# An expert stage that adds its rows in PSUM, reads the fullest expert's weights once, and loads down weights from ScalarE's queue

## The reference, cut to what matters

```python
# hier_moe: top-1 of 4 groups, then top-2 of its 8 experts; weight = p(group) * softmax of the two
hb = jax.nn.silu(xb @ w_gate[e]) * (xb @ w_up[e])        # 1024 -> 512, for each chosen (token, expert)
y  = (hb @ w_down[e]) * wr[:, None]                      # 512 -> 1024
h  = h + segment_sum(y, row_tok)                         # both experts of a token, on the residual
y_prompt, y_sample = rmsnorm(h, final_norm_g)
```

## Time and profile before

| | us |
|---|---|
| median of 3 runs | 1508.8 (1507.97 to 1509.42) |
| the profiled execution | 1504.2 |
| its span on the core | 1502.6 |
| PE busy | 1150.9 (77%) |
| DVE busy | 464.5 (31%) |
| ACT busy | 234.5 (16%) |
| POOL busy | 207.2 (14%) |
| bytes moved | 315.69 MB, 210 GB/s over the span |

### The profile page before, as it was taken

How to read it: one execution, slowest core, us unless ns; L and a number is a source line. 1 busy time by engine, 2 the same in 40 slices (tenths; PEclk the granted TensorE clock), 3 DMA queues, 4 the chain that set the end, 5 groups by cost and what they waited for, 6 DMA issues and landing times. The chain is left out here.

```text
span 1502.6 us, 22749 instructions
## 1 busy us (share of the span) xinstructions
PE 1150.9 (77%) x7953; PEld 729.8 (49%) x7953; DVE 464.5 (31%) x1117; ACT 234.5 (16%) x646; POOL 207.2 (14%) x402
## 2 busy tenths in 40 slices
PE   5899999999995898877899999666565656565650
PEld 3666667666763455554566664443232333232320
DVE  2235654656455574333000001331111111111113
ACT  1132233223322353222000000000000000000000
POOL 3033433344324111010000000000000000000003
PEclk9799999999997998999899999678887888787875
DMA  6033424332422226542965360299999999999963
GB/s 197 20 113 88 115 84 143 104 99 84 143 59 56 51 49 175 133 148 84 255 155 134 80 232 0 77 413 426 429 428 428 428 427 429 429 427 428 428 283 123
DMA packets 171882, 315.69 MB, mean 210 GB/s; under 512 B 22162, under 2 KB 153810, under 8 KB 159170
## 3 DMA queue, kind: packets, MB, share of 16 engines
q1 hardware_dynamic: 161842, 303.34, 56.1%
q0 software_dynamic: 2048, 6.95, 1.6%
q10 hardware_dynamic: 7952, 4.88, 1.1%
HBM read 296.02 MB, written 19.11 MB: 210 GB/s over the span
## 5 line engine op out<-in xcount | busy, mean ns | idle before, releaser
L1696 PE MATMUL ph<-w_gate_up,x_gathered 128*32 128x256 f32 x1408 | 121.8, 521 | 108.7 <-DMA w_gate_up<-in_w_exp_up 108.1
L669 PE MATMUL psg<-stretch 128*128 128x336 f32 x512 | 159.8, 477 | 11.3 <-DVE h_sample_out L647 9.6
L1696 PEld LDWEIGHTS ph<-w_gate_up,x_gathered 128*32 128x32 f32 x1408 | 60.5, 148 | 170.1 <-issue 98.1
L669 PEld LDWEIGHTS psg<-stretch 128*128 128x128 f32 x512 | 103.7, 204 | 69.2 <-DVE h_sample_out L647 15.4
L1664 DVE SCALAR_TENSOR_TENSOR h_gate<-h_tanh,ph 128x128 f32<-128x128 f32 x33 | 9.5, 287 | 387.3 <-ACT h_tanh L1624 387.3
L1696 PE MATMUL ph<-stretch,x_gathered 128*32 128x256 f32 x704 | 60.7, 519 | 57.9 <-DMA stretch<-in_w_exp_up 57.9
L584 DVE SCALAR_TENSOR_TENSOR x_conv<-x_padded,conv_wh,x_conv 128x360 f32<-128x360 f32 x96 | 56.9, 593 | 101.0 <-ACT x_conv L533 90.0
L678 PE MATMUL psg<-stretch 128*128 128x256 f32 (+1 forms) x384 | 84.5, 380 | 0.0
L1346 PE MATMUL psm<-stretch,w_merge 128*128 128x336 f32 x256 | 75.8, 455 | 6.9 <-DMA w_merge<-in_w_in 6.9
L1745 POOL DMA_INDIRECT y_expert<-expert_rows,slot_i x6 | 5.7, 958 | 505.8 <-PEq L1715 504.2
L678 PEld LDWEIGHTS psg<-stretch 128*128 128x128 f32 (+1 forms) x384 | 67.3, 177 | 14.5
(11 more groups left out here) (415 smaller groups left out, 1659.4 us busy)
## 6 DMA issues: line engine op xcount, KB each, us to landing
w_down<-in_w_exp_down SPq DMA_DIRECT2D x33, 2048.0 KB, 40.4
w_gate_up<-in_w_exp_gate SPq DMA_DIRECT2D x22, 2048.0 KB, 33.8
w_gate_up<-in_w_exp_up SPq DMA_DIRECT2D x22, 2048.0 KB, 38.4
stretch<-in_w_exp_gate SPq DMA_DIRECT2D x11, 2048.0 KB, 34.1
stretch<-in_w_exp_up SPq DMA_DIRECT2D x11, 2048.0 KB, 38.7
stretch<-in_w_in SPq DMA_DIRECT2D x16, 1024.0 KB, 5.3
stretch<-in_w_in SPq DMA_DIRECT2D x16, 512.0 KB, 7.5
h<-in_state_ssm SPq DMA_DIRECT2D x16, 512.0 KB, 4.8
```

The source lines that it names most:

```text
L669: mm = pe.matmul(ps[m][:, 0:T], wg[:, k, P * m:P * m + P], S["xnT"][:, k, :], start=(k == 0), stop=(k == KT - 1))
L1696: mm = pe.matmul(ph[h][32 * j:32 * j + 32, 0:256], xg[h][:, k, :], w_gu[w][:, :, k, P * j:P * j + P], start=(k == 0), stop=(k == KT - 1))
```

## The change

- The residual and the expert rows are summed in six PSUM banks (`acc`, "token_rows"). TensorE first puts the residual there with an identity (six matmuls at the start of routing), then, for each block, adds the block's rows with 12 matmuls: 32 rows of `back`, which holds the router weight where a token has this slot, times 32 rows of `y_block`. `expert_rows`, its blank write, its stores and its gather are gone, and so is `final_phase`: the norm reads the banks at the end of `moe_phase`, after six closing matmuls with zeros.
- Routing also spreads each token's two slots and two weights over all partitions as rows: products with the identity (VectorE and GpSimd), 12 matmuls with `ones`, four copies by ScalarE. VectorE makes `back` for each block from them.
- There are always 33 blocks. The fullest expert among 3 to 31 takes block 28 (the expert of that number goes to its place), and its pairs 33 to 64 are block 31, which computes with the weights that block 28 loaded; expert 31 is block 32. Overflow blocks beyond begin at 33. Every load takes its expert's number from `blk_e`.
- Down weights are issued by ScalarE, for block b + 3 after the copy of block b; gate and up stay with SyncE.
- `ph`'s two halves share one bank, `px` and `py` another.
- The loops: 4 x 6 blocks, blocks 24 to 32 written out, then 4 x 6 bodies under an If from block 33.

The diff, cut to its core:

```diff
+NMAIN = NE + 1
+TWICE, AGAIN = 28, 31
 NOVER = 20
-NBLK = NE + NOVER
+NBLK = NMAIN + NOVER
+ADD_ORDER = [(0, 0), (0, 1), (0, 2), (0, 3), (1, 0), (1, 1), (1, 2), (1, 3), (2, 0), (2, 2), (2, 1), (2, 3)]
...
-            sp.wait_ge(kx_ok, 1)
-            sp.dma_start(S["ydram"][NE * BLK:SLOTS, :].rearrange("(b p) d -> p b d", p=64),
-                         bc(blank[0:64].unsqueeze(1), [64, (SLOTS - NE * BLK) // 64, D])).then_inc(blank_out, 16)
...
-            v.memset(blank, 0.0)
...
 def route_phase(nc, A, S, sem):
...
+            for j in range(2):
+                pool.tensor_tensor(dgw[:, j, :, :], bc(S["ident"][:, :].unsqueeze(1), [P, 3, P]),
+                                   bc(S["topw"][:, :, j:j + 1], [P, 3, P]), ALU.mult).then_inc(dgw_ok, 1)
...
+            for j in range(2):
+                act.wait_ge(row_ps, j + 1)
+                act.activation(S["slot_row"][:, j, :], ps[j][:, 128:128 + T], ACT.Copy).then_inc(row_ev, 1)
+            for j in range(2):
+                act.wait_ge(row_ps, j + 3)
+                act.activation(S["weight_row"][:, j, :], ps[j][:, 128:128 + T], ACT.Copy).then_inc(row_ev, 1)
...
+            for j in range(4):
+                pe.matmul(acc[:, j, :], S["ident"][:, :], S["xtok"][:, 0:2, 256 * j:256 * j + 256],
+                          start=True, stop=False)
+            for i in range(2):
+                pe.matmul(acc[0:80, 4 + i, :], S["ident"][0:80, 0:80], S["xtok"][0:80, 2, 512 * i:512 * i + 512],
+                          start=True, stop=False)
             pe.wait_ge(mk, 1)
...
+            for src, ok, freed in ((dgs, dgs_ok, 0), (dgw, dgw_ok, 2)):
+                for j in range(2):
+                    pe.wait_ge(ok, j + 1)
+                    if freed:
+                        pe.wait_ge(row_ev, j + 1)
+                    for t, r in enumerate(ROWS):
+                        mm = pe.matmul(ps[j][:, 128 + COL[t]:128 + COL[t] + r], o[0:r, :], src[0:r, j, t, 0:r],
+                                       start=True, stop=True)
+                    mm.then_inc(row_ps, 1)
...
+            for j in range(2):
+                v.tensor_tensor(dgs[:, j, :, :], bc(S["ident"][:, :].unsqueeze(1), [P, 3, P]),
+                                bc(S["slot"][:, :, j:j + 1], [P, 3, P]), ALU.mult).then_inc(dgs_ok, 1)
...
 def moe_phase(nc, A, S, sem):
...
+        def loads(b):
+
+            return b // 3 + 1 - (1 if b >= AGAIN and b % 3 == AGAIN % 3 else 0)
+
         def each_block(eng, nblk, body):
-            sure = NE // UNROLL
+            sure = TWICE // UNROLL
             with eng.Fori(0, sure) as i:
                 for u in range(UNROLL):
-                    body(UNROLL * i + u, u, i)
-            with eng.Fori(sure, -(-NBLK // UNROLL)) as i:
+                    body(UNROLL * i + u, u, 2 * i + loads(u))
+            for b in range(sure * UNROLL, NMAIN):
+                body(b, b, loads(b))
+            with eng.Fori(0, -(-NOVER // UNROLL)) as i:
                 for u in range(UNROLL):
-                    with eng.If(UNROLL * i + u < nblk):
-                        body(UNROLL * i + u, u, i)
+                    with eng.If(UNROLL * i + u + NMAIN < nblk):
+                        body(UNROLL * i + u + NMAIN, u + NMAIN, 2 * i + loads(u + NMAIN), over=True)
...
                 act.wait_ge(y_ps, b + 1)
-                act.wait_ge(y_sent[h], 64 * (3 * i + u // 2) + 64)
-                act.activation(yr[h][:, :], py[h][:, 0:256], ACT.Copy).then_inc(y_ev, 1)
-                act.drain()
-                for j in range(4):
-                    act.dma_start(ydram[bass.ds(BLK * b, BLK), j, :], yr[h][32 * j:32 * j + 32, :]
-                                  ).then_inc(y_sent[h], 16)
+                act.wait_ge(added, b + 1)
+                act.activation(yr[h][:, :], py[:, :], ACT.Copy).then_inc(y_ev, 1)
+                def refill(column):
+                    e = act.value_load(S["blk_e"][0:1, column], min_val=0, max_val=NE - 1)
+                    load_down(act, A, S, u % 3, e)
...
+            def weights_back(b, h):
+                v.scalar_tensor_tensor(weq[:, :, :], slot_row[:, :, :], lane[:, 0:1], weight_row[:, :, :],
+                                       ALU.is_equal, ALU.mult)
+                v.drain()
+                v.wait_ge(added, b + 1)
+                v.tensor_tensor(back[h][:, :], weq[:, 0, :], weq[:, 1, :], ALU.add).then_inc(back_ok, 1)
+                v.tensor_scalar(lane[:, :], lane[:, :], float(BLK), None, ALU.add)
...
                 gather_rows(b + 2, 1 - h)
                 pe.wait_ge(ht_ok, b + 1)
-                pe.wait_ge(dn_in[w], 32 * i + 16 * (u // 3) + 16)
-                pe.wait_ge(y_ev, b)
+                pe.wait_ge(xt_ok, b + 2)
+                pe.wait_ge(dn_in[w], 16 * n)
+                pe.wait_ge(y_ev, b + 1)
...
                 mm.then_inc(y_ps, 1)
+                pe.wait_ge(y_ev, b + 2)
+                pe.wait_ge(back_ok, b + 1)
+                for t, j in ADD_ORDER:
+                    r, q = ROWS[t], slice(32 * j, 32 * j + 32)
+                    if (t, j) == (2, 1):
+                        mm.then_inc(tail_half, 1)
+                        pe.wait_ge(tail_half, b + 1)
+                    mm = pe.matmul(token_rows(t, j), back[h][q, COL[t]:COL[t] + r], yr[h][q, :], start=False,
+                                   stop=False)
+                mm.then_inc(added, 1)
...
+            for i in range(6):
+                r = P if i < 4 else 80
+                mm = pe.matmul(acc[0:r, i, 0:CLOSE], S["zeros"][:, 0:r], S["ident"][:, 0:CLOSE], start=False, stop=True)
+            mm.then_inc(all_added, 1)
```

More of the change, by code:

```diff
@@ L901, in _ @@
                     load_kv(2 * i + half, half, True)
-            sp.wait_ge(blank_out, 16)
         @block.gpsimd
@@ L1515, in _ @@
+            v.tensor_copy(rank[0:80, 2, :], ps[0][0:80, 64:96])
+            v.drain()
+            v.tensor_scalar(most[:, :], key[:, :], topn[:, 0:1], None, ALU.is_equal)
+            v.tensor_reduce(nb[:, :], over[:, :, :], AX.X, ALU.add)
+            v.drain()
+            v.tensor_tensor(far2[:, :], most[:, :], over[:, :, 0], ALU.mult)
+            v.tensor_tensor(key[:, :], most[:, :], to28[:, :], ALU.mult)
             v.tensor_scalar(late[:, :, :], rank[:, :, :], BLK - 0.5, None, ALU.is_gt)
@@ L1578, in moe_phase @@
+        pw = [ctx.enter_context(nc.psum_tensor(f"pw{h}", [P, 512], F32)) for h in range(2)]
+        ph = [pw[0][:, 256 * h:256 * h + 256] for h in range(2)]
+        px, py = pw[1][:, 0:256], pw[1][:, 256:512]
         sel_ok, xr_ps, xt_ok, gu_ps, th_ok, hb_ok, ht_ok, y_ps, y_ev = (
             sem(n) for n in ("sel_ok", "xrow_ps", "xt_ok", "gu_ps", "hth_ok", "h_ok", "ht_ok", "yb_ps", "yb_ev"))
-        y_sent = [sem("y_sent_even"), sem("y_sent_odd")]
-        ydram = S["ydram"].rearrange("s (j d) -> s j d", j=4)
+        back_ok, added, all_added, tail_half = (sem("weights_back_ok"), sem("rows_added"), sem("all_added"),
+                                                sem("tail_half_added"))
@@ L1619, in _, with body @@
             nblk = blocks_of(act)
-            def body(b, u, i):
+            act.dma_start(fg[:, :], A["final_norm_g"].partition_broadcast(P)).then_inc(g_in, 16)
+            def body(b, u, n, over=False):
                 h = u % 2
@@ L1625, in body @@
                 act.wait_ge(y_ps, b + 1)
-                act.wait_ge(y_sent[h], 64 * (3 * i + u // 2) + 64)
-                act.activation(yr[h][:, :], py[h][:, 0:256], ACT.Copy).then_inc(y_ev, 1)
-                act.drain()
-                for j in range(4):
-                    act.dma_start(ydram[bass.ds(BLK * b, BLK), j, :], yr[h][32 * j:32 * j + 32, :]
-                                  ).then_inc(y_sent[h], 16)
-            act.sem_inc(y_ev, 1)
-            act.sem_inc(y_sent[0], 64)
-            act.sem_inc(y_sent[1], 64)
-            each_block(act, nblk, body)
-            for h in range(2):
-                act.wait_ge(y_sent[h], 64 * ((nblk + (1 - h)) // 2) + 64)
-                act.sem_inc(S["pool_passed"])
+                act.wait_ge(added, b + 1)
[3 more added lines that the diff above has]
+                    load_down(act, A, S, u % 3, e)
+                if isinstance(b, int) and b + 3 < NMAIN:
+                    if b + 3 != AGAIN:
+                        refill(slice(b + 3, b + 4))
+                elif isinstance(b, int):
+                    with act.If(b + 3 < nblk):
+                        refill(slice(b + 3, b + 4))
+                elif u < TWICE // UNROLL * UNROLL and not over:
+                    refill(bass.ds(b + 3, 1))
+                else:
+                    with act.If(b + 3 < nblk):
+                        refill(bass.ds(b + 3, 1))
+            act.sem_inc(added, 2)
+            act.sem_inc(y_ev, 1)
+            each_block(act, nblk, body)
+            act.wait_ge(all_added, 1)
+            for t in (2, 0, 1):
+                r = ROWS[t]
+                act.activation(as_tile(xsq[0:r, :], t), tile_rows(t), ACT.Square,
```

(2 more changed lines are left out.)

264 lines of the change are left out of this document (155 added, 109 removed).

## The result

| | before | after |
|---|---|---|
| median, us | 1508.4 (1506.9 to 1509.4, 4 runs) | 1575.8 (1569.7 to 1578.7, 4 runs) |
| span of the profiled execution, us | 1502.6 | 1577.0 |
| PE busy, us | 1150.9 | 1216.0 |
| bytes moved, MB | 315.69 | 300.54 |

The changed kernel is slower: ratio 1.044, 95% interval [1.041, 1.048]. The forecast was 1492.7, faster. Lines are those of the changed kernel: gate/up L1868, gather L1858, down L1878, the adds L1888, the closing matmuls L1896.

The account below looks back on a forecast made before the run. The expert stage was taken as bound by weight transfers, the last blocks by TensorE. TensorE's end 1454.2 + 33.3 - 1.0 gave span 1486.5, 16.1 below 1502.6; from the median 1508.8, 1492.7 us, range 1484 to 1504.

Parts of the forecast that it names:

- The end: After TensorE's last block: skipped bodies 16.6 us, closing matmuls 2.4, the rest 14.3; 33.3 in place of 43.4, -10.1.
- the list of signs: What would show the forecast right or wrong: loads, queue rate, waits, block and add times, the gap before the closing matmuls.
- 1.0 for attention: Attention: VectorE's memset of the blank rows goes, from the path to TensorE's first matmul there: -1.0 us.
- Last blocks: Blocks 30 to 32: one load left but three blocks of 10.5 us; with 1.5 for landing order TensorE ends at 1454.2.
- The rival in which the tail hides: Last blocks: TensorE catches up and ends one block after the last byte, 8 us earlier, 1485; chance 0.12.
- The down-queue term: Expert stage: down loads on their own queue run ahead, so gate/up lands later by 0 to 4.9 us, 1.5 taken.
- Routing: Before the first refill: VectorE +4.0, residual +0.3, row products +6.2, warmer clock -1.5; refill at 1007.8, queue empty +8.7 us.
- Traffic: Expert stage's queue: one 6.29 MB load less, -14.7 us, and no 32 KB row stores, -10.1 us.
- The adds: Each block on TensorE: 12 adds, 24 passes, with four row groups overlapping, take 2.4 us; block 10.3, with slack 10.5.
- adds in a row: Rival for each block's adds: row groups don't overlap, block 13.9 us, last three cost 10.2 more, 1503; chance 0.12.
- TensorE as the bound: Rival for the expert stage: adds of 6.3 us make blocks 14.2; at 15 us a block, 1536, slower; chance 0.05.
- the load was dropped: Expert stage: the fullest expert's two blocks share one load; the rival that it isn't dropped gives 1500, chance 0.03.

Follow-up runs that it names:

- the one with nine adds: The changed kernel with nine adds of twelve in the bodies of its never-run second loop: 1577.7 us, one run.
- the versions with both edits: Changed kernel, one test ahead of the second loop, fullest expert at places 24 and 27, down loads on SyncE's queue: 1474.2 us; with TensorE's sure blocks written out, 1472.9.
- the version without the jumps: Changed kernel with one test, early pair, down loads on SyncE's queue, and TensorE's 24 sure blocks written out in place of a loop: 1472.9 us, ratio 0.977.
- its two versions: The kernel before with its second loop as two turns of twelve bodies, 1556.4 us; and with a test around each turn of that loop, 1502.5 us.

## Why the prediction was wrong

It failed in one step above all: *"The end. Skipping 21 bodies took up to 14.5 us, 0.69 each; now 24 are skipped: 16.6 (to 20 if it goes by TensorE's larger body)."* It measured 94.75 us. The row was read as a price per body and carried over by count. It held two things: 21 skips at about 0.32, and, as the rest, fetches of code. And that price holds only while the loop stays in what the sequencer keeps; the change made the body 12 matmuls longer, and no row of before showed where that ends. The bound from above, 20 us, took the length of the body for a factor; it should have asked what a loop of 72 matmuls a body costs if it is fetched in each turn. The trace of before had the means: 24 packets on the instruction queue, two of them in a window otherwise nearly empty. The Trainium skill (Advanced Engine Details and Errata, ISA Cache) gives TensorE a cache of 128 KB for its instructions, in lines of 16 KB; the prediction didn't draw on it. The trace agrees with the lines: the packets are of 16 KB. The size fits as far as the runs go: a loop of some 108 KB was kept, and one that takes 8 packets a turn, at most 128 KB, was not; the one with nine adds, some 123 KB by the estimate above, was not either, so the usable size lies below that or the estimate is off. No rival had it, though the list of signs named it ("more than 17 us between the last add and the closing matmuls").

The steps, from the forecast span of 1486.5 to the 1577.0 measured:

| step | forecast, us | measured, us | difference on the path |
|---|---|---|---|
| block 29's gate/up starts on TensorE | 1421.7 (for block 30's) | 1425.3 | +3.6 |
| blocks from there to the last add | 3 x 10.5 | 44.4, four blocks | +12.9 |
| skipped bodies | 16.6 | 94.75 | +78.2 |
| closing matmuls | 2.4 | 2.4 | 0 |
| from there to the end | 14.3 | 10.2 | -4.1 |

(1421.7 is the forecast's 1435.9 - 14.7 + 1.5 with its 1.0 for attention taken off.) With one test ahead of the loop the first row is 1422.7 and the third 3.1, and the sum is 1482.9, that version's span, 3.6 below the forecast of 1486.5. That is luck: the first two rows are 13.9 us over the forecast there, and stepping over the loop, which the forecast didn't have, is 13.5 under it. The rest of the working, without the loop, was 12.4 us too low for the changed kernel.

The first row also holds something from ahead of the stage: the first weight load went out at 974.98, 6.8 us later than the 968.22 of the earlier trace rows, where the prediction had 1.0 sooner. What of it is the change isn't shown (last section). Two sums are slightly off, too: the terms of the last row give 14.4, not 14.3, and from 999.2 to 1007.8 is 8.6, not 8.7.

*Last blocks.* The second term was wrong in its mechanism: "only one load, block 32's, is left, 14.7 us, but three blocks". At 1425.3 the 8.3 MB still to move were 6.3 for block 32 and so at most 2.0 of block 30's 6.3: two thirds of that load had come by the time block 29's gate and up were there. TensorE had block 29, half of it at the lower clock (gate/up 6.54 us), and three more. The rival in which the tail hides is the state that the versions with both edits reach, one block after the last load. The down-queue term, "0 to 4.9, I take 1.5", was undersized: moving the down loads back let block 29 start 9.3 us sooner, of which 6.0 reached the end of TensorE.

*Routing.* From the first weight load of the stage to the first refill it took 974.98 to 1013.12, 38.1 us, against 30.6 before: +7.5 where +9.0 was forecast. The row products took 996.19 to 1001.4, 5.2 us and 5.7 with the last copy, where 6.2 was taken; that was at a granted clock of 0.53, so doubling the warm price to 8.1 us was too dear. The first block came up cold (5.65 us), so the 1.5 us for a warm clock was not there. It came elsewhere: behind the residual's matmuls the nine rank matmuls ran at the full clock (granted 1.00 instead of 0.50, 1.9 us instead of 3.6), and VectorE's chain began 9.9 us into the stage, not 11.5 as in the earlier trace rows.

```profile
974.98 0.33 SPq L1629 DMA_DIRECT2D w_gate_up<-in_w_exp_gate  x1
...
1007.27 5.65 PE L1868 MATMUL pw<-w_gate_up,x_gathered 128*32 128x256 f32 x64 [0.64 <-DVE x_gathered L1802]
...
1013.12 0.34 SPq L1629 DMA_DIRECT2D w_gate_up<-in_w_exp_gate  x1
```

*Traffic.* Right: 32 down loads and no stores; 29 of the loads come from ScalarE's queue and the first three from SyncE's. The 15.15 MB less on the page are 6.29 of weights, 4.3 of stores, the gathers and the blank write, less 1.1 MB of code; 426 GB/s where 428 was taken.

*The adds.* Right: 2.29 us for 24 passes, forecast 2.4, so the four row groups do overlap, and a block that waits for nothing takes 1459.36 - 1449.10 = 10.3, forecast 10.3 with slack 10.5. That also settles three rivals: adds in a row would show 5.8, TensorE as the bound needed 6.3, and the load was dropped. The Trainium skill (TensorEngine Tiling (Array Packing), Tiling Modes) has a drain at each change of tiling mode; the 0.4 us kept for two of them fits in these 2.29 us, and no run here measures it alone.

```profile
1467.40 2.29 PE L1888 MATMUL token_rows<-y_block,weights_back 32*128 32x256 f32 x24 [0.49 <-ACT y_block L1756]
```

*The end behind the closing matmuls* was 4.1 us shorter: GpSimd's two operations took 0.19 and 0.56 us, not the 2.6 taken from the earlier trace rows, and the three squares ran one behind the other under them.

## What to carry to other kernels

A loop in which nothing runs isn't free: its code is still stepped through, and on TensorE, once the loop was longer than what the sequencer keeps, it was fetched again in each turn, here at 2.9 us per 16 KB. Put one test around a rare loop, and when a change lengthens an unrolled body, look at the instruction queue's packets, not only at the engine's busy time. Where a load is saved, ask what the queue carries while the engine uses the old one; put the saved load where other loads can fill the time, not at the end.

## What the runs showed beyond that

The same refetching appears in the steady stretch of the changed kernel: 29 packets from 1010 to 1300 us where before has 4, with a stall of 5.7 to 7.0 us at each of the three jumps back. It stayed hidden under the transfers: the same matmuls still wait 67 us for weights besides, and in the version without the jumps these waits grew by what the stalls had been.

The start of the router's matmuls, ahead of which the edits tried here change nothing, fell at 959.4 to 959.5, 962.4 to 962.7 or 965.1 to 965.5 us in seven of the versions built on the changed kernel, steps of 3 us (966.2 and 967.2 in the last two), and at 958.3 to 959.9 in before and its two versions. 3 us is what one fetch of code costs here, but the fetches up to 960 us number 12 in before, in the changed kernel and in each version of it that was counted, so what makes the steps stays open. They are also the size of the spread between runs of one kernel (before: 1500.7 to 1511.6 in the comparisons of the first seven versions), and bound what a single run can tell. The forecast 1.0 us for the dropped memset can't be read from them.
